# Hymba-style streaming step on one core: the two smallest experts go last, 125 rows each, both multiplied token by token, and the token sums are fetched while the last one runs

## What is computed

```python
def hier_moe(x, w_rg, b_rg, w_re, b_re, w_gate, w_up, w_down):
    """Top-1 expert group, then top-2 experts within it; gated-MLP experts."""
    ...
    for e in range(N_EXPERTS):
        hid = jax.nn.silu(x @ w_gate[e]) * (x @ w_up[e])
        y = y + gates[..., e:e + 1] * (hid @ w_down[e])
    return y
...
    x = x + mix @ w_out
    x = x + hier_moe(rmsnorm(x, norm2_g), w_rg, b_rg, w_re, b_re, w_gate, w_up, w_down)
...
    y_prompt = rmsnorm(xp, norm_f_g)
    y_sample = rmsnorm(xs, norm_f_g)
```

## Time and profile before

| | us |
|---|---|
| median of 3 runs | 938.84 (938.76 to 940.09) |
| span of the profiled execution | 939.7 |
| busy in it: PE, DVE, POOL, ACT | 880.8, 431.1, 374.6, 154.5 |
| PE's last matmul ends at about | 908.15 |
| last instruction of any engine starts at | 932.03 |

### The profile page before, as it was taken

How to read it: one execution, slowest core, us unless ns; L and a number is a source line. 1 busy time by engine, 2 the same in 40 slices (tenths; PEclk the granted TensorE clock), 3 DMA queues, 4 the chain that set the end, 5 groups by cost and what they waited for, 6 DMA issues and landing times.

```text
span 939.7 us, 16689 instructions
## 1 busy us (share of the span) xinstructions
PE 880.8 (94%) x6339; PEld 755.1 (80%) x6339; DVE 431.1 (46%) x1166; ACT 154.5 (16%) x456; POOL 374.6 (40%) x576
## 2 busy tenths in 40 slices
PE   5989999999999999999989799999999999999960
PEld 3974987869588695886945699999999999999920
DVE  3144474645646456463557843333333333333264
ACT  2031212121311213111131210000000000000071
POOL 4040031210302103021150258767767776777524
PEclk9989999999999999999999899999999999999985
DMA  9930203030110301003027389999999999999883
GB/s 328 280 151 1 68 1 80 12 79 1 28 52 1 79 1 34 25 1 57 1 62 291 71 294 299 327 352 335 360 346 333 327 322 326 315 319 314 248 305 115
DMA packets 90039, 163.15 MB, mean 174 GB/s; under 512 B 48887, under 2 KB 59027, under 8 KB 81770
## 3 DMA queue, kind: packets, MB, share of 16 engines
q1 hardware_dynamic: 70062, 136.43, 41.5%
q0 software_dynamic: 17728, 25.28, 11.2%
q10 hardware_dynamic: 2188, 0.59, 0.3%
HBM read 139.83 MB, written 25.87 MB: 176 GB/s over the span
## 4 chain that ended last, share of the span: by engine, by line
PE 51%; DMA 16%; issue 11%; POOL 11%; DVE 9%; ACT 1%; POOLq 1%; DVEq 0%; SPq 0%; ACTq 0%
PE bank L1527 48%; DMA z_d<-wout,win 12%; POOL z_d L599 7%; DVE wout L1443 2%; POOL wout L551 2%; PE bank L1532 1%; DVE wout L1436 1%; DVE win L1482 1%; DMA wout<-h_d,idt 1%; DMA h2T<-z_d 1%; DVE win L1407 1%; PE bank L1732 0%; DMA xbuf<-in_x_prompt 0%; POOL pad L595 0%; PE bank L1645 0%
## 5 line engine op out<-in xcount | busy, mean ns | idle before, releaser
L1527 PE MATMUL bank<-wout,win 128*128 128x150 f32 (+3 forms) x2048 | 246.3, 282 | 1.1 <-DVE wout L1129 1.1
L1527 PEld LDWEIGHTS bank<-wout,win 128*128 128x128 f32 x2048 | 244.7, 190 | 1.2 <-DVE wout L1129 1.2
L1527 PE MATMUL bank<-hT,win 128*128 128x128 f32 (+1 forms) x1536 | 182.9, 279 | 0.0
L1527 PEld LDWEIGHTS bank<-hT,win 128*128 128x128 f32 x1536 | 178.6, 192 | 1.5 <-issue 1.2
L1527 PE MATMUL bank<-win 128*128 128x130 f32 (+5 forms) x1024 | 137.3, 294 | 2.7 <-DVE win L1428 1.4
L599 POOL DMA_INDIRECT z_d<-wout,win x75 | 125.2, 1669 | 27.1 <-issue 26.8
L1527 PEld LDWEIGHTS bank<-win 128*128 128x128 f32 (+2 forms) x1024 | 125.5, 191 | 12.3 <-issue 10.3
L1527 PE MATMUL bank<-win,hT 128*128 128x260 f32 (+3 forms) x512 | 122.2, 417 | 3.0 <-DVE xbuf L1247 1.5
L1527 PE MATMUL bank<-wout,mixT 128*128 128x512 f32 (+1 forms) x384 | 116.8, 487 | 1.8 <-ACT mixT L845 1.7
L1527 PEld LDWEIGHTS bank<-win,hT 128*128 128x128 f32 (+1 forms) x512 | 77.1, 173 | 43.0 <-issue 34.1
L1436 DVE STREAM_TRANSPOSE wout<-bank 128x480 f32<-128x480 f32 (+1 forms) x45 | 25.1, 603 | 156.7 <-DMA z_d<-wout,win 155.2
(11 more groups left out here) (308 smaller groups left out, 812.0 us busy)
## 6 DMA issues: line engine op xcount, KB each, us to landing
win<-in_w_gate SPq DMA_DIRECT2D x32, 1024.0 KB, 6.3
win<-in_w_up SPq DMA_DIRECT2D x32, 1024.0 KB, 9.2
win<-in_w_down SPq DMA_DIRECT2D x32, 1024.0 KB, 10.6
win<-in_w_in SPq DMA_DIRECT2D x4, 2048.0 KB, 20.1
xbuf<-in_x_prompt SPq DMA_DIRECT2D x8, 512.0 KB, 3.8
wout<-in_w_out SPq DMA_DIRECT2D x1, 4096.0 KB, 15.6
z_d<-xbuf SPq DMA_DIRECT2D x32, 128.0 KB
h_d<-xn SPq DMA_DIRECT2D x8, 512.0 KB, 2.7
```

The costliest lines, as they stand in the source:

```text
L1527: return nc.tensor.matmul(out, lhsT, rhs, start=first, stop=last)
```

## The change

Order and size: the two smallest experts are taken out of the third and fourth place and put last. The places are now r = 30, 30, four times 26, twice 27, twice 28, four times 30, twice 25. The table that DVE works out gets some ten small instructions more (`order`, `more`, `ends`, `behind`), so that further blocks, where there are any, come ahead of the last two. POOL prepares one more size at the program's start (`RS`).

Block 15 is now by token too, in one piece of 125 (`FN`), as is block 16. Neither is added to `z_d`. Instead, with the token numbers of both blocks (`fid`, `lid`, eleven small transfers that ACT starts) DVE makes a 125 x 125 matrix `same` that says which token of block 16 is one of block 15's, and a column `away` that keeps such a row of block 15 from being written. Block 15's gated outputs (`ygr`) are added to gathered sums and normed on the chip, and two further products `same` x `ygr` put block 15's share into block 16's rows.

Fetching: SP no longer waits for block 15's rows. It waits for `added` of block 14 and fetches four tiles (`GROUPS[0]`), then the last half of the down weights, then five tiles. On ACT, block 16's `silu` stands behind the four tiles' squares, with two more table loads around it. On DVE, block 16's `products` stand behind block 15's sums, the norm of the first group and the output of two tiles. POOL weighs two tiles (`WEIGHED`) while block 16 runs. SP starts the stores of the nine tiles. The norm's weight `nfg` is loaded before the expert loop.

The diff, cut to its core:

```diff
-    SLOTS = ((30, 1), (30, 1), (26, 6), (27, 2), (28, 2), (30, 2))
+    SLOTS = ((30, 1), (30, 1), (26, 4), (27, 2), (28, 2), (30, 2))
+    LR, FX = 25, NE - 2
+    SIZES = [NP * r for r, n in SLOTS for _ in range(n)] + [BLOCK] * (FX - NS) + [NP * LR] * 2
...
+        FN = NP * LR
+        FBANK = ((7, 1), (5, 6))
+        WEIGHED = (2, 3)
...
-        GROUPS = (range(0, 2), range(2, 5), range(5, NT))
+        GROUPS = (range(0, 4), range(4, 7), range(7, NT))
...
 # SP
+            sp.wait_ge(gu_done, 4 * nblocks)
+            load_gate_up(e, 1)
+            sp.wait_ge(d0_used, nblocks)
+            load_down(e, 0)
+            sp.wait_ge(added, 16 * NP * (sooner + 1))
+            for t in GROUPS[0]:
+                fetch_sums(t)
+            sp.wait_ge(last_done, EARLY_DOWN + 2)
+            load_down(e, 1)
+            for t in range(len(GROUPS[0]), NT):
+                fetch_sums(t)
...
 # POOL
-            add_block(sooner + 2, RP, 7 * sooner + 13)
...
-            pool.wait_ge(added, 16 * NP * (sooner + 2))
+            pool.wait_ge(added, 16 * NP * (sooner + 1))
...
+            for at, t in enumerate(WEIGHED):
+                pool.wait_ge(scaled, at + 1)
+                g.tensor_tensor(yb[t], yb[t], nfg, ALU.mult).then_inc(weighed, 1)
...
 # ACT
+            for t in GROUPS[0]:
+                squares(t)
+            start_norm(fs0, GROUPS[0][0], GROUPS[0][-1] + 1)
+            act.preload_act_table_set("silu_and_others")
...
+                a.activation(sgl[:, f % 2, 0:n], B[GB[f]][:, 0:n], ACT.Silu).then_inc(silu_ready, 1)
+                if f == 0:
+                    act.wait_ge(mixed, FIRST_NORMS)
...
+            act.preload_act_table_set("natural_log_exp_and_others")
+            for t in GROUPS[1]:
+                squares(t)
...
 # DVE
+            norms(0)
+            v.memset(fs[:, 4, 0:1], 0.0).then_inc(mixed, 1)
+            outputs(t for t in GROUPS[0] if t not in WEIGHED)
+            products(nblocks, LR)
...
+            norms(1)
+            outputs(GROUPS[1])
+            for c in range(2):
+                cols = slice(c * (D // 2), (c + 1) * (D // 2))
+                dve.wait_ge(last_done, LAST_DOWN + c + 1)
+                last = v.scalar_tensor_tensor(out=fy[0][0:FN, cols], in0=B[FBANK[0][c]][0:FN, :], scalar=fid[0:FN, 0, 1:2],
+                                              in1=fy[0][0:FN, cols], op0=ALU.mult, op1=ALU.add)
...
+            rstd(GROUPS[2][0], NT + 1)
+            outputs(GROUPS[2])
...
 # PE
+            gate_up(sooner + 2, LR)
+            down_by_token(sooner + 2, 1)
+            gate_up(nblocks, LR, False)
+            pe.wait_ge(away_ready, 1)
+            for c in range(2):
+                pe.wait_ge(ygr_ready, c + 1)
+                mm(B[FBANK[1][c]][0:FN, :], same[0:FN, :], ygr[0:FN, c * (D // 2):(c + 1) * (D // 2)]).then_inc(last_done, 1)
+            down_by_token(nblocks, 0)
```

298 lines of the change are left out of this document (170 added, 128 removed).

## The result

The changed kernel takes 944.81 us (median of 6 runs, 942.47 to 947.81) against 940.3 for the kernel before (median of 6). The ratio is 1.0053, 95% interval 1.0037 to 1.0068: it is slower by about half a per cent. Over all the runs made beside the experiments the kernel before had medians of 940.2 to 940.9. The prediction was 933.7 us, 927.5 to 939.0, with 0.8 for faster; it missed the sign and the range.

What follows compares the result with a forecast made beforehand. PE bounds blocks up to 908, then a chain from block 14's landing (875.4) through tile 3 (889.5), block 16's products (900.6), last outputs (918.0) and stores (922.1), plus 12.5: span 934.6, time 933.7 us, range 927.5 to 939.0.

Steps and rivals of the forecast that it cites:

- Block 3's start: PE's start of block 3, taken at 583.39 us from the earlier profile as base for the later times.
- The order of blocks: PE, blocks 3 to 14: they take 274.2 us in the new order, block 14 ending at 857.5, 4.4 us later.
- Blocks 15 and 16: PE's last blocks: gate and up 13.8 us at 125 columns, down product 7.1; unheld end at 901.1, 7 us before 908.15.
- Block 14 in memory: Landing of block 14's added rows, 14.6 + 3.3 us after PE's end of the block, at 875.4; the fetches wait for it.
- The rival that the chain stays behind: Chain adding rows to memory still lags at block 14: landing at 883.5, time 941.8 us; chance 0.19, of it 0.08 slower.
- Tile 3: Arrival of the fourth fetched tile of sums: 10.8 us after the first fetch plus 3.3 for queued weights, at 889.5.
- The clash: DVE outputs held beside POOL's weighing, ahead of block 16's products: 4.5 us, bounds 0 and 4.5.
- The half clock for the last product: PE's clock falling while it waits: last product ends at 914.7 instead of 907.7, the sum 1.7 us higher.
- The two table loads: ACT's extra table loads around block 16's silu: 1.3 us each; with the skill's drain the sum would be 2.7 us higher.
- The tail: From the last stores' landing to the end of the span: 12.5 us, as in the kernel before.
- From the profile to the median: Profiled span of 934.6 us turned into a median time: 0.9 us less, 933.7.
- slow rival: Memory chain stays behind, chance 0.19; over 0.2% slower when tile 3 arrives 7 us late, after 896.5.

Runs made afterwards that it cites:

- the second profile: The changed kernel, unchanged, profiled once more: block 3 starts at 581.89, tile 3 squared 20.8 us after the first fetch, tail 14.9 us.
- e13_lr24: Changed kernel with products first, norm's weights in PSUM, group 1's squares ahead of scaled copies, and 120 places instead of 125 in the last two blocks: 934.63 us.
- e14_late_order: Changed kernel with both gathers started after tile 3's landing and VectorE's sums of block 15 moved behind the last expert's products: 939.48 us, 0.9989.
- e9_gathers_late: Changed kernel with GpSimd starting both gathers of base rows only once tile 3's sums have landed: 951.8 us, 1.0113.
- e3_no_weigh: Changed kernel with tiles 2 and 3 written by DVE behind block 16's products, instead of ScalarE's scaled copy and POOL's weighing: 940.54 us, 0.9999.
- e12_rows_120: Changed kernel with two gathers and four last scatters over the first 120 of 125 places, some tokens left out: 942.44 us, 1.0015.
- e7_tail_30: Changed kernel with one of the last two experts' final scatters by token writing 30 of its 125 rows: 946.52 us, 1.0067.

## Why the prediction was wrong

From profile to profile the forecast was a span of 934.6, and it came to 944.5.

- **Block 3's start**, taken over as 583.39, was 585.01: +1.6. It belongs to this one execution; the second profile has 581.89.
- **The order of blocks: right.** 273.94 us against 274.2, no wait of PE in blocks 7 to 12, as said.
- **Blocks 15 and 16: nearly right.** Gate and up take 14.29 us at 125 columns (858.95 to 873.24), as at 130, not 13.8; e13_lr24 has 14.45 for the 128 records at 120 columns too. The line through the 130 and 150 columns of the earlier trace rows doesn't go on downward. Over the two blocks this is 1 us, hidden behind PE's wait for the products. The down product by token took 6.87 us against 7.1.
- **Block 14 in memory: right.** First fetch at 877.39, against 875.4 + 1.6. The memory chain had caught up by block 13: block 14's results wait for PE and no longer for a landing, as VectorE's timeline shows. The rival that the chain stays behind is refuted, though the kernel is slower.

```profile
856.59 0.68 DVE L1512 STREAM_TRANSPOSE wout<-bank 128x480 f32<-128x480 f32 x1 [3.59 <-PE bank L1627]
```

- **Tile 3: the step that failed.** Forecast 14.1 us after the fetch, measured 19.7 (897.1 - 877.4); with 0.4 us ahead of it this makes +6.0. The term "I take 3.3 us more" set the rate at 321 to 415 GB/s from the earlier trace rows and counted only what stands in SP's queue. GpSimd's two gathers moved forward with the fetches, and the traffic of these gathers stands nowhere in the sum. With them out of the way (e14_late_order) it is 14.0 us, the forecast's own number. That it is this close is in part luck: e9_gathers_late, with the gathers out of the way too, has 15.0.
- **The clash: right.** Price 4.5 us forecast, 4.3 measured (e3_no_weigh). From tile 3 to the products 11.1 us were forecast (900.6 - 889.5); they came 10.2 us behind it, at 907.35. The half clock for the last product came too: it takes 9.45 us where block 15's took 7.03. It cost nothing, since it ends at 917.3 and VectorE's sums that read it start at 919.50. The Trainium skill (TensorE: Matmul & The Clock Gate, "HAM oscillation"), which lets the clock fall in waits between bursts, was right on the clock: the granted clock is 0.50 from 900 to 904, while PE stands. The 1.7 us that the sum would have taken for it aren't there.
- **The two table loads: right.** The SiLU at 900.21 follows the load at 898.91, which takes 1.28 us, 0.02 us after its end. The drain of about 1.4 us that the Trainium skill (ScalarE: Activation LUTs, "What ACT_TABLE_LOAD costs") gives on top isn't seen.
- **The tail: mis-sized.** "Then 12.5 as now" became 15.1: +2.6. I took the tail over without costing the four scatters again, which went from 120 and 30 rows to 125 each. 1.4 us of it is the row count (13.7 us with 120 rows, e12_rows_120). Where the other 1.2 us come from isn't shown: the scatters move more than before, but in e7_tail_30, where they move less, the tail is no shorter.
- **From the profile to the median.** I put the median 0.9 us below the span of the profile, as it was for the kernel before. For the changed kernel it lies 0.3 above: the profiled execution took 946.4 us for its span of 944.5, and the median is 1.6 us below that, 944.81. This adds 1.2 us. The 0.9 itself was chance: an execution's time lies about 2 us above its span (944.09 for 942.2), and the median of three runs that I had, 938.84, was some 1.4 us low against the later 940.2.

The sum: 934.6 + 1.6 + 6.0 + 2.6 - 0.3 for the small ones (10.2 us and not 11.1 from tile 3 to the products, 22.1 and not 21.5 from there to the stores' landing) = 944.5; with the last point 933.7 + 9.9 + 1.2 = 944.8.

The range failed for the same reason as the sum. Its slow rival had the right trigger, "it becomes slower than before when tile 3 arrives 7 us late, after 896.5" (897.1 measured), but only one way to get there, the memory chain; the shared rate was no case of its own.

## What to carry to other kernels

Of a stage that is moved, add up the traffic of all queues that will run beside it, and take its rate from a stretch of the trace in which the same queues are active, not from the best stretch. Where a row count of an indirect transfer can be chosen, look at the share of DMA engines it gets: here 120 rows were twice as fast as 125. And if two edits each clear one of two things that hold the same engine, try them together before dropping either.
